# One 512-column product over the high and low halves in three 256-column stages, a projection taken chunk by chunk, and a second bank for turns

## The reference

```python
def conv_ffn(h, w_up, conv_w, conv_b, w_down):
    ug = dwconv3(h @ w_up, conv_w, conv_b)
    u, g = jnp.split(ug, 2, axis=-1)
    return (jax.nn.silu(g) * u) @ w_down
...
    for l in range(DEPTH):                    # first block
        x = x + gt1_x * (jnp.concatenate([oa, ob, oc], axis=-1) @ w_out[l])
        hx2 = modulate(rms_norm(x, g_norm2[l]), sh2_x, sc2_x)
        x = x + gt2_x * conv_ffn(hx2, w_up[l], conv_w[l], conv_b[l], w_down[l])
...
    for l in range(DEPTH):                    # second block
        h = h + 0.5 * rmsnorm(swiglu(rmsnorm(h, g_pre_ffn1[l]), w_ffn1_gu[l], w_ffn1_down[l]), g_post_ffn1[l])
        mix = token_mixer(rmsnorm(h, g_pre_mix[l]), ...)     # ends in y @ w_out
        h = h + rmsnorm(mix, g_post_mix[l])
        h = h + 0.5 * rmsnorm(swiglu(rmsnorm(h, g_pre_ffn2[l]), w_ffn2_gu[l], w_ffn2_down[l]), g_post_ffn2[l])
    return h[:, BLOCK:]
```

## Time and profile before

| | |
|---|---|
| median of 3 runs | 2416.02 us (2408.54 to 2417.76) |
| the profiled execution | 2414.93 us |
| its span | 2413.1 us |
| TensorE busy | 2324.8 us, 96%, 17349 matmuls |
| VectorE busy | 1563.3 us, 65% |
| ScalarE busy | 1198.0 us, 50% |
| mean granted TensorE clock | 0.986 |

### The profile page before, as it was taken

The page is one execution under the profiler, slowest core; times in us unless marked ns, Lnnn a source line. Parts: engine busy times, 40 slices in busy tenths (PEclk is TensorE's granted clock), DMA queues, the critical chain, the costliest instruction groups (busy, mean ns, idle before and its releaser), DMA issues.

```text
span 2413.1 us, 46839 instructions
## 1 busy us (share of the span) xinstructions
PE 2324.8 (96%) x17349; PEld 2118.5 (88%) x17349; DVE 1563.3 (65%) x2789; ACT 1198.0 (50%) x2055; POOL 144.9 (6%) x252
## 2 busy tenths in 40 slices
PE   7999999999999999999999999999999999998998
PEld 5787778888877889999999889899999998898998
DVE  5436579887885467875665755676566557565764
ACT  4537534444236455654444555554454455655553
POOL 1214300000100120000000000000000000000000
PEclk9999999999999999999999999999999999998999
DMA  8750025444644114555555334455545553353664
GB/s 302 225 174 20 33 99 166 147 140 142 201 137 145 53 39 145 177 177 162 186 173 174 112 101 138 149 165 174 170 147 184 166 162 117 102 167 124 201 182 128
DMA packets 101200, 356.44 MB, mean 148 GB/s; under 512 B 11344, under 2 KB 13040, under 8 KB 101072
## 3 DMA queue, kind: packets, MB, share of 16 engines
q1 hardware_dynamic: 86704, 304.45, 40.0%
q0 software_dynamic: 14368, 50.24, 6.5%
HBM read 352.55 MB, written 1.05 MB: 147 GB/s over the span
## 4 chain that ended last, share of the span: by engine, by line
PE 84%; DVE 7%; ACT 4%; issue 3%; DMA 1%; DVEq 0%; ACTq 0%; SPq 0%; POOL 0%
PE ps L768 22%; PE ps L770 22%; PE ps L769 22%; DVE wl L1775 3%; PE ps L785 2%; PE ps L786 2%; PE ps L916 2%; PE ps L789 2%; PE ps L931 2%; PE ps L902 2%; ACT wh L1316 1%; DVE conv L2392 1%; PE ps L836 1%; DMA ada_raw<-in_w_ada 1%; PE ps L1184 1%
## 5 line engine op out<-in xcount | busy, mean ns | idle before, releaser
L1775 DVE TENSOR_TENSOR wl<-raw,wh 128x1024 fp32r<-128x1024 f32 x574 | 701.1, 1222 | 459.2 <-ACT wh L1316 458.5
L768 PE MATMUL ps<-hH,wh 128*128 128x272 f32 (+2 forms) x2864 | 885.1, 309 | 6.2 <-DVE silu L2447 3.1
L769 PE MATMUL ps<-hL,wh 128*128 128x272 f32 (+2 forms) x2864 | 871.1, 304 | 0.0
L770 PE MATMUL ps<-hH,wl 128*128 128x272 f32 (+2 forms) x2864 | 870.8, 304 | 0.0
L1316 ACT ACTIVATE wh<-raw 128x1024 fp32r<-128x1024 f32 x574 | 602.6, 1053 | 328.8 <-PE ps L770 303.5
L768 PEld LDWEIGHTS ps<-hH,wh 128*128 128x128 f32 x2864 | 542.8, 190 | 37.9 <-issue 7.2
L769 PEld LDWEIGHTS ps<-hL,wh 128*128 128x128 f32 x2864 | 542.9, 190 | 19.8 <-issue 0.5
L770 PEld LDWEIGHTS ps<-hH,wl 128*128 128x128 f32 x2864 | 543.1, 190 | 19.0
L768 PE MATMUL ps<-actH,wh 128*128 128x272 f32 (+2 forms) x1136 | 344.0, 303 | 3.0 <-DVE wl L1775 2.0
L770 PE MATMUL ps<-actH,wl 128*128 128x272 f32 (+2 forms) x1136 | 345.5, 304 | 0.0
L769 PE MATMUL ps<-actL,wh 128*128 128x272 f32 (+2 forms) x1136 | 343.0, 302 | 0.0
(11 more groups left out here) (306 smaller groups left out, 2950.6 us busy)
## 6 DMA issues: line engine op xcount, KB each, us to landing
raw<-in_w_ffn_gu SPq DMA_DIRECT2D x176, 512.0 KB, 3.5
raw<-in_w_mix SPq DMA_DIRECT2D x98, 512.0 KB, 3.5
raw<-in_w_up SPq DMA_DIRECT2D x88, 512.0 KB, 3.5
raw<-in_w_ffn_down SPq DMA_DIRECT2D x64, 512.0 KB, 3.6
ada_rest<-in_w_ada POOLq DMA_DIRECT2D x32, 512.0 KB, 4.6
raw<-in_w_out SPq DMA_DIRECT2D x32, 512.0 KB, 3.5
raw<-in_w_down SPq DMA_DIRECT2D x32, 512.0 KB, 3.6
raw<-in_w_qk SPq DMA_DIRECT2D x26, 512.0 KB, 4.4
```

The costliest lines, as they stand in the source:

```text
L768: pe.matmul(out, a_h, b_h, start=start, stop=False)
L769: pe.matmul(out, a_h, b_l, start=False, stop=False)
L770: return pe.matmul(out, a_l, b_h, start=False, stop=stop)
L1775: dve.tensor_tensor(wl[:, slot, :], raw[:, slot, :], wh[:, slot, :].bitcast(F32), ALU.subtract).then_inc(l_split, 1)
```

## The change

In `out1`, `down1` and `up2_1` the high-weight product runs once over both activation halves, 512 columns wide, into a full bank: high by high to its first half, high by low to its second. The low-weight product adds 256 columns to the first half. Whoever reads the tile adds the two halves: `add_gated` with a second instruction, the evictions of `up2_1` with a `tensor_reduce` over the two, with the multiplication by the root as a separate instruction behind it. The Silu waits for that one. `first_group` keeps its three matmuls and sends the low half to the second half of the bank. `hH`, `hL` and `actH`, `actL` become views of one tensor each.

`out_0` and `out_1` drop `first_group`; their first chunk waits for the activation tiles k by k, the others follow. In layer 1 of the first block turns alternate between banks 5 and 7, and a turn waits for the rope two before it.

The diff, without the semaphores' declarations and the call sites that only pass `wide`:

```diff
+        hHL = sb("hHL", [P, 2, KT, T1], F32R)
+        hH, hL = hHL[:, 0], hHL[:, 1]
...
+        def rot_bank(l, i):
+            return 7 if l and ropes_before[i] % 2 else 5
...
+            def product_wide(bank, a_h, a_l, both, high, start, stop):
+
+                if start:
+                    pe.matmul(ps[:, bank, :], a_h, both, start=True, stop=False)
+                last = pe.matmul(ps[:, bank, 0:TX], a_l, high, start=False, stop=False)
+                if not start:
+                    last = pe.matmul(ps[:, bank, :], a_h, both, start=False, stop=stop)
+                return last
...
             def first_group(...):
-                        pe.matmul(ps[:, bank, lo:T], w_h, src[0][:, k, lo:T], start=k == 0, stop=False)
-                        pe.matmul(ps[:, bank, lo:T], w_l, src[0][:, k, lo:T], start=False, stop=False)
+                        out = ps[:, bank, 0:TX] if wide else ps[:, bank, lo:T]
+                        pe.matmul(out, w_h, src[0][:, k, lo:T], start=k == 0, stop=False)
+                        pe.matmul(out, w_l, src[0][:, k, lo:T], start=False, stop=False)
...
-                        last = pe.matmul(ps[:, bank, lo:T], tile_w(slot, k)[0], src[1][:, k, lo:T], start=False, stop=k == KT - 1)
+                        out = ps[:, bank, TX:2 * TX] if wide else ps[:, bank, lo:T]
+                        last = pe.matmul(out, tile_w(slot, k)[0], src[1][:, k, lo:T], start=False, stop=k == KT - 1)
...
             def feature_major(...):
+                    first = latest if latest and isinstance(s.j, int) and s.j == 0 else {}
+                    order = [k for k in range(KT) if k not in first] + sorted(first)
                     for k in order:
+                        for ready, count in first.get(k, ()):
+                            pe.wait_ge(ready, count)
+                        if wide:
+                            last = product_wide(bank, *tile_w(slot, k), hHL[:, :, k, lo:T], src[0][:, k, lo:T],
+                                                k == order[0], k == order[-1])
...
             def down(...):
+                        if wide:
+                            last = product_wide(bank, *tile_w(slot, k), actHL[:, :, kk, lo:T], src[0][:, kk, lo:T],
+                                                kk == 0, kk == FT - 1)
...
-                    if ropes_before[i]:
-                        pe.wait_ge(roped, roped_by(l, i) - 1)
-                    pe.matmul(ps[:, 5, 0:TX], ...)
+                    if ropes_before[i] > l:
+                        pe.wait_ge(roped, roped_by(l, i) - 1 - l)
+                    pe.matmul(ps[:, rot_bank(l, i), 0:TX], ...)
...
-                first_group(S[f"out_{l}"], merge_h, merge_l, 8 * l, (actH2, actL2), lo=lo)
-                feature_major(S[f"out_{l}"], T2, (actH2, actL2), skip=GROUP, lo=lo)
+                feature_major(S[f"out_{l}"], T2, (actH2, actL2), peel=1, lo=lo,
+                              latest={k: ((merge_h, 8 * l + k + 1), (merge_l, 8 * l + k + 1)) for k in range(KT)})
...
                     if s.k % 2 == 0:                                   # ScalarE, silus
-                        act.wait_ge(bank_free[bank], s.over(st.g0, 4) + 2)
+                        if st.name == "up2_1":
+                            act.wait_ge(gate_scaled, pair + 1)
+                        else:
+                            act.wait_ge(bank_free[bank], s.over(st.g0, 4) + 2)
...
                         last = dve.scalar_tensor_tensor(x, ps[:, bank, t0:t0 + tn], g, x, ALU.mult, ALU.add)
+                    if l == 1:
+                        link(last)
+                        last = dve.scalar_tensor_tensor(x, ps[:, bank, TX:2 * TX], g, x, ALU.mult, ALU.add)
                     last.then_inc(bank_free[bank], 1)
...
+                        wide = which == 2 and l == 1
+                        halves = ps[:, bank, :].rearrange("p (h t) -> p t h", h=2)
                         if s.k % 2 == 0:
+                            if wide:
+                                dve.tensor_reduce(silu2[:, r, lo:], halves, AX.X, ALU.add).then_inc(bank_free[bank], 1)
+                                dve.wait_ge(bank_free[bank], s.over(st.g0, 4) + 2)
+                                dve.tensor_tensor(silu2[:, r, lo:], silu2[:, r, lo:], rstd, ALU.mult).then_inc(gate_scaled, 1)
...
+                        if wide:
+                            dve.tensor_reduce(act32b[:, r, lo:], halves, AX.X, ALU.add).then_inc(bank_free[bank], 1)
...
                         dve.wait_ge(bank_free[bank], s.over(st.g0, 4) + 2)
+                        if wide:
+                            dve.tensor_tensor(act32b[:, r, lo:], act32b[:, r, lo:], rstd, ALU.mult).then_inc(value_scaled, 1)
+                            dve.wait_ge(value_scaled, pair + 1)
                         dve.wait_ge(silu_ready, p0 + pair + 1)
                         dve.tensor_tensor(act32b[:, r, lo:], act32b[:, r, lo:], silu2[:, r, lo:], ALU.mult).then_inc(act32_ready, 1)
```

More of the change, by code:

```diff
@@ L201, in build_program @@
         arena = top[0]
-        actH = sb("actH", [P, FT, T1], F32R)
-        actL = sb("actL", [P, FT, T1], F32R)
+        actHL = sb("actHL", [P, 2, FT, T1], F32R)
+        actH, actL = actHL[:, 0], actHL[:, 1]
         ffn_top = top[0]
@@ L800, in feature_major @@
                     pe.wait_ge(bank_free[bank], s.over(st.g0, 4) + 1)
[L801 to L804, removed]
+                    first = latest if latest and isinstance(s.j, int) and s.j == 0 else {}
+                    order = [k for k in range(KT) if k not in first] + sorted(first)
                     for k in order:
[L806 to L809, removed]
+                        for ready, count in first.get(k, ()):
[4 more added lines that the diff above has]
+                        else:
+                            last = product(ps[:, bank, lo:T], *tile_w(slot, k), src[0][:, k, lo:T], src[1][:, k, lo:T],
+                                           k == order[0], k == order[-1])
                         if mid and isinstance(s.j, int) and s.j == skip and k == 5:
@@ L862, in fold_sums, with down @@
                 last.then_inc(ada_turned, 1)
-            def down(st, T, src, p0, lo=0):
+            def down(st, T, src, p0, lo=0, wide=False):
                 for s in steps(pe, st.n, 12):
@@ L873, in down @@
                             pe.wait_ge(actL_ready, p0 + (FT - 2 if kk == 0 else kk + 1))
-                        last = product(ps[:, bank, lo:T], *tile_w(slot, k), src[0][:, kk, lo:T], src[1][:, kk, lo:T],
-                                       kk == 0, kk == FT - 1)
+                        if wide:
+                            last = product_wide(bank, *tile_w(slot, k), actHL[:, :, kk, lo:T], src[0][:, kk, lo:T],
+                                                kk == 0, kk == FT - 1)
+                        else:
+                            last = product(ps[:, bank, lo:T], *tile_w(slot, k), src[0][:, kk, lo:T], src[1][:, kk, lo:T],
+                                           kk == 0, kk == FT - 1)
                     last.then_inc(chunk_used, 1)
@@ L1079, in _ @@
                 pe.wait_ge(diff_l, 2 * (l + 1))
-                feature_major(S[f"out{l}"], tq, peel=1, after=None if l else widen, latest=(PAIRS[-1], pair_l, 6 * (l + 1)))
+                feature_major(S[f"out{l}"], tq, peel=1, wide=l == 1, after=None if l else widen, latest={PAIRS[-1]: ((pair_l, 6 * (l + 1)),)})
                 n = norms["n2", l]
@@ L1084, in _ @@
                 feature_major(S[f"up{l}"], tq, skip=GROUP)
-                down(S[f"down{l}"], tq, (actH, actL), pair0[f"up{l}"])
+                down(S[f"down{l}"], tq, (actH, actL), pair0[f"up{l}"], wide=l == 1)
                 if l == 0:
@@ L2445, in ffn @@
                         wait_tile(st, s)
+                        wide = which == 2 and l == 1
+                        halves = ps[:, bank, :].rearrange("p (h t) -> p t h", h=2)
                         if s.k % 2 == 0:
-                            dve.tensor_tensor(silu2[:, r, lo:], ps[:, bank, lo:T2], rstd,
-                                              ALU.mult).then_inc(bank_free[bank], 1)
+                            if wide:
+                                dve.tensor_reduce(silu2[:, r, lo:], halves, AX.X, ALU.add).then_inc(bank_free[bank], 1)
+                                dve.wait_ge(bank_free[bank], s.over(st.g0, 4) + 2)
+                                dve.tensor_tensor(silu2[:, r, lo:], silu2[:, r, lo:], rstd, ALU.mult).then_inc(gate_scaled, 1)
+                            else:
+                                dve.tensor_tensor(silu2[:, r, lo:], ps[:, bank, lo:T2], rstd,
+                                                  ALU.mult).then_inc(bank_free[bank], 1)
                             continue
```

22 lines of the change are left out of this document (12 added, 10 removed).

## The result

The changed kernel takes **2436.0 us** (median of 5 runs, 2429.3 to 2445.7), the kernel before 2416.0 (5 runs, 2408.5 to 2418.7): ratio 1.009, 95% interval 1.0071 to 1.0110, so 17 to 27 us slower. The forecast was 2429 us, with a range of 2414 to 2440. The profiled execution took 2440.07 us.

What follows compares the result with a forecast made beforehand. TensorE looked the bound, with a VectorE-ScalarE loop hidden in `up2_1` that the change would expose. Terms 23.4 - 0.3 - 2.0 - 7.5 - 0.6 = +13.0 on 2414.9 gave 2427.9, plus 1.1 for the median, 2429 us; range 2414 to 2440.

Steps and rivals of the forecast that it cites:

- The bound: In `up2_1`, VectorE and ScalarE form a loop of 5.17 us a pair, hidden under TensorE's 5.65 with 0.48 to spare.
- Rival 1: TensorE stays the bound in `up2_1`, gaining 2.9 us in place of losing 23.4: 2402.7 us; chance 0.12.
- The length of the loop: Longer `up2_1` evictions take the loop from 5.17 to 6.62 us a pair (gate +0.72, value +0.73), net +23.4 us.
- Rival 2: The strided reduce in `up2_1`'s evictions is slow, 1.22 us: 1.06 more a pair, 2451 us; chance 0.05.
- The start of `down2_1`: At `down2_1`'s fourth chunk, TensorE's own work covers 2.4 us of the delay from `up2_1`, within the net +23.4 us.
- Rival 5: The clock falls in loop-bound `up2_1`, where TensorE idles 17% of the time: a few us, 2432 us; chance 0.04.
- The wide product: A step falls from 0.360 to 0.347 us: `out1` net -0.3, `down1` -2.0, 2.9 in `up2_1` if TensorE sets the pace.
- Rival 4: The wide matmul saves nothing: 3.1 us more, 2432 us; chance 0.05.
- The projection: `out_0` and `out_1`, started chunk by chunk, wait less and `out_1` keeps its clock: net -2.3 and -5.2 us.
- The turns: In layer 1, TensorE's turn no longer waits for the rope before it: -0.6 us, bounds 0 and -1.5.
- Own waits: In `up2_1` evictions, each wait of VectorE for its own result costs 0.12 us.
- rival 3: Own waits in `up2_1` are free, 0.12 us less twice a pair: 5.0 less, 2424 us; chance 0.05.

Runs made afterwards that it cites:

- split_first: The changed kernel with ScalarE's split of the value tile's chunk issued ahead of the gate tile's Silu in `up2_1`: 2404.3 us, ratio 0.9952 to the kernel before.
- up2_wide_only: The kernel before with the wide product and its evictions in `up2_1` alone, and the layout: 2442.9 us, ratio 1.0106.
- no_wait_for_reduce: The changed kernel with the `up2_1` reduces writing an unread tile, so no TT waits for a reduce: 2435.4 us, ratio 1.0077 to the kernel before.
- value_wide_only: The changed kernel with only the value tiles of `up2_1` wide, gate tiles as before the change: 2418.5 us, ratio 1.0023 to the kernel before.
- the control: The kernel before with the tiles laid out anew and every instruction otherwise as before: 2416.9 us, ratio 1.0000.
- before_split_first: The kernel before with ScalarE's split of the value tile's chunk ahead of the Silu in `up1_0`, `up2_0`, `up1_1`, `up2_1`: 2415.2 us, ratio 1.0001.
- up2_narrow: The changed kernel with `up2_1` computed as before (three 256-column products a step, one TT as eviction): 2405.4 us, ratio 0.9963 to the kernel before.

## Why the prediction was right, point by point

- **The bound.** Right: a loop of VectorE and ScalarE, hidden with 0.48 us a pair to spare, became the bound. `split_first` shows it by opening the loop. Rival 1 (TensorE stays the bound) is refuted, though it is what the kernel becomes once the order is changed.
- **The length of the loop.** Forecast 6.62, measured 6.70. The gate side was right (0.72 forecast, 0.73 measured): reduce 0.68, Silu 1.18 behind the reduce (forecast 0.69 and 1.17). Rival 2 (slow reduce) falls. The value side was priced 0.08 short: the product behind the scaling TT starts 0.54 later (2298.63 to 2299.17), not 0.45. It waits for two semaphores, its own and the Silu's, and I had priced one; that the second one is the reason is not shown by a run of its own. 20 periods make 1.6 us.
- **The start of `down2_1`: the step that failed.** The sum had 2.4 us covered there by TensorE's own work. The cover was there (the fourth chunk started 22.3 later, its split 24.5), but I did not ask what the clock does when TensorE has idled at the start of a stage. The three profiled kernels with the full loop (`up2_wide_only` and `no_wait_for_reduce` besides the changed one) show the lower level there, and so does `value_wide_only`, which has the same wait of 2.5 us (0.72 over the 6 us from 2348). Rival 5 looked for this in `up2_1`, where the clock stayed at 1.00 with weights loading for 21.4 of 30 us; I had the price right (about 3 us) and the place wrong. With 1.9 for the longer loop this is the 4.7 us by which the line was short, and the larger part of it.
- **The wide product.** Direction right, size too large. It saves 0.008 us a step in `down1`, where the sum had 0.013, and 0.004 in `up2_1`, where it had 0.009 (2.9 us over 328 steps). What was mis-sized is the pair of a wide and a narrow matmul: the forecast added the pace of a stretch with 512 columns alone to that of one with 256 alone, 0.347 in `down1` and 0.344 in `up2_1`, and measured are 0.350 and 0.349. In `down1` it also took 0.120 for a narrow matmul, where the earlier trace rows count 0.119. Rival 4 (it saves nothing) falls too, but only half of the saving is there. The formula of the Trainium skill (TensorE: Matmul & The Clock Gate, Back-to-back issue gap), which the page gives for a matmul by itself and not for a stream with a weight load for each, would have given 0.6 us for TensorE's part of `out1` and `down1` where I had 3.1; their 240 steps at 0.008 make 1.9, so the measurement lies between the two.
- **The projection.** Right in size (-7.3 against -7.5), in the wait that is left (1.34 against 1.2) and in the clock; the control shows that the clock's part (2.6 us) is likely, not certain.
- **The turns.** At the wrong end of my bounds: 0, as the argument about a loop without TensorE already said. I should have kept to it.
- **Own waits.** 0.13 where 0.12 was priced; rival 3 falls.
- The total: 20.0 us between the medians where 13.0 were forecast. Of the 7, 6.3 come from the edited parts (19.3 - 13.0, without the -1.2): 4.7 from the loop and the clock at `down2_1`, 0.5 from `down1`, 0.6 from the turns, and 0.4 from `out1` and the projection, but for rounding. The other 0.7 lie inside the interval of the ratio.

## What to carry to other kernels

Before making the evictions of an engine longer, look whether two engines wait only for each other: then their instructions along the cycle add up to a period, whatever share each is busy, and the spare time against TensorE's period is the whole budget. Such a cycle often comes from the order on a queue, here a weight split queued behind a Silu that has to wait; moving the independent instruction ahead added no work and made a change that lost 20 us gain 11. Where TensorE will wait at the start of a stage, count a slower clock behind the wait as possible: it came in four of four kernels behind 2.5 us at `down2_1`, in five of six behind 3.3 at `out_1`, in none of six behind 2.5 at `out_0`.

## What was not expected of the hardware

The same matmuls run at more than one steady pace with the granted clock at 1.00. In `up2_1`, `before_split_first` issues the very matmuls of the kernel before, but 268 in 30 us in place of 257. By the distances between evictions, 5.44 and 5.65 us for 48, that is 0.113 us each and not 0.118:

```profile
2290.00:2320.00 30.00, 30.00 (x268) 30.00 (x267) 21.63 (x34) 15.43 (x24) 0.00 (x0) 1.00 0.61 193
```

Its `up2_1` came out 4.6 us shorter, mostly by that. In the 272-column stages a pair takes either 6.02 or 6.08 us, and the same stage of the same code was seen with both in different kernels (`up1_1`: 6.08 before, 6.02 in `up2_narrow`), a step of about 1 us a stage. What picks the pace, no run here tells; the 5.44 stands in this kernel alone, so that the new order brings it is not excluded. Stages without an edit differ by 1 to 3.5 us, by the pace as in `up1_1` or by the clock as in `v0` and `up0`, and that may be why single edits of 1 to 7 us came through in the stages but not fully in whole times.
